# Down products as seven block products per pair of tiles, with GpSimd making the weight sums and part of the low parts

## What is computed

```python
def mlp(h, w_up, w_down):
    return jnp.square(jax.nn.relu(h @ w_up)) @ w_down
```

## Time and profile before

| | us |
|---|---|
| median of 3 runs | 1792.21 (1791.98 to 1797.71) |
| span of the profiled execution | 1793.1 |
| PE busy | 1736.8 (97%), 15035 matmuls |
| DVE busy | 954.7 (53%) |
| ACT busy | 548.6 (31%) |
| POOL busy | 159.4 (9%) |
| first MLP, second MLP after its root | 397.0 each |

### The profile page before, as it was taken

One profiled execution on the slowest core, in us unless ns is written; L12 is line 12 of the kernel. 1 busy time (PEld: TensorE's weight loads), 2 busy tenths in 40 slices (PEclk: granted clock), 3 DMA queues, 4 the chain that ended last, 5 costly groups with the idle time before them and its releaser, 6 DMA issues.

```text
span 1793.1 us, 36785 instructions
## 1 busy us (share of the span) xinstructions
PE 1736.8 (97%) x15035; PEld 1623.3 (91%) x15035; DVE 954.7 (53%) x1454; ACT 548.6 (31%) x1075; POOL 159.4 (9%) x212
## 2 busy tenths in 40 slices
PE   7998999999999999999999999999999999999998
PEld 6995667899999999999898898878799999999998
DVE  4336776655353433444587774677665435343454
ACT  4114556432121222231511413443133212122222
POOL 0710000320000000020000000012012000000002
PEclk9999999999999999999999999999999999999999
DMA  8219999337676767544368678523033767422221
GB/s 277 71 50 363 351 353 346 124 118 257 234 257 234 257 233 257 187 131 158 96 198 284 211 253 274 197 83 102 33 121 120 278 227 260 173 79 88 75 91 55
DMA packets 167162, 338.82 MB, mean 189 GB/s; under 512 B 9178, under 2 KB 116500, under 8 KB 165437
## 3 DMA queue, kind: packets, MB, share of 16 engines
q1 hardware_dynamic: 164691, 249.74, 41.3%
q0 software_dynamic: 2240, 87.41, 13.0%
q10 hardware_dynamic: 114, 0.03, 0.0%
HBM read 324.36 MB, written 100.19 MB: 237 GB/s over the span
## 4 chain that ended last, share of the span: by engine, by line
PE 86%; DVE 7%; ACT 2%; DMA 2%; issue 1%; SPq 1%; ACTq 0%; DVEq 0%
PE pp L667 55%; PE pp L977 16%; PE pp L727 2%; PE pp L926 1%; DMA kvring<-in_cache_b_kv 1%; PE pp L741 1%; PE pp L761 1%; PE pp L1084 1%; PE pp L1131 1%; PE pp L1180 1%; PE pp L1109 1%; DVE stat L1668 1%; DVE pp L1666 1%; ACT e_p L2163 1%; DMA vring<-in_cache_d_kv 1%
## 5 line engine op out<-in xcount | busy, mean ns | idle before, releaser
L1943 ACT ACTIVATE whi<-raw 128x1024 fp32r<-128x1024 f32 x208 | 220.6, 1060 | 899.7 <-PE pp L667 687.7
L667 PE MATMUL pp<-a_hi,whi 128*128 128x288 f32 x1280 | 275.8, 297 | 1.0 <-DVE zbuf L1335 0.7
L667 PE MATMUL pp<-a_lo,whi 128*128 128x288 f32 x1280 | 274.6, 296 | 0.0
L667 PE MATMUL pp<-a_hi,wlo 128*128 128x288 f32 x1280 | 274.4, 296 | 0.0
L1292 DVE TENSOR_TENSOR wlo<-raw,whi 128x1024 fp32r<-128x1024 f32 x208 | 256.0, 1231 | 30.5 <-ACT whi L1943 30.4
L667 PE MATMUL pp<-b_hi,whi 128*128 128x288 f32 x1152 | 247.0, 296 | 0.0
L667 PE MATMUL pp<-b_lo,whi 128*128 128x288 f32 x1152 | 247.0, 296 | 0.0
L667 PE MATMUL pp<-b_hi,wlo 128*128 128x288 f32 x1152 | 246.9, 296 | 0.0
L1351 DVE TENSOR_TENSOR x<-x,pp 128x576 f32 (+1 forms) x80 | 60.4, 755 | 295.1 <-PE pp L667 284.0
L667 PEld LDWEIGHTS pp<-a_hi,whi 128*128 128x128 f32 x1280 | 206.6, 189 | 2.3 <-issue 1.7
L667 PEld LDWEIGHTS pp<-a_lo,whi 128*128 128x128 f32 x1280 | 206.7, 189 | 0.0
(11 more groups left out here) (304 smaller groups left out, 2062.9 us busy)
## 6 DMA issues: line engine op xcount, KB each, us to landing
kvring<-in_cache_b_kv SPq DMA_DIRECT2D x128, 512.0 KB, 5.6
out_new_d_sample<-in_cache_d_kv POOLq DMA_DIRECT2D x32, 2040.0 KB, 8.5
raw<-in_w_up SPq DMA_DIRECT2D x32, 1024.0 KB, 5.4
raw<-in_w_down SPq DMA_DIRECT2D x32, 1024.0 KB, 5.2
kring<-in_cache_d_kv SPq DMA_DIRECT2D x104, 256.0 KB, 3.3
vring<-in_cache_d_kv SPq DMA_DIRECT2D x104, 256.0 KB, 5.3
raw<-in_w_in_cd SPq DMA_DIRECT2D x24, 1024.0 KB, 5.2
out_new_d_sample<-in_cache_d_kv POOLq DMA_DIRECT2D x8, 2016.0 KB, 8.3
```

What stands on the lines that cost most here:

```text
L667: last = pe.matmul(acc_h[s][:, h, :], w[s][:, k, :], m[:, k, NH * h:NH * h + NH], start=(at_ == 0 and n == 0), stop=(at_ == KT_N - 1 and n ...
L1943: act.activation(whi_v[j], raw_v[q // 2][:, :, j, :], ACT.Copy).then_inc(whi_ready, 1)
```

## The change

The 8 output tiles of a down half are taken in 4 pairs. For a pair, the weights (8 k-tiles by 2 tiles) are seen as a 2 by 2 block matrix (halves of k, and the two tiles), and the squares as 2 by 2 (halves of k, halves of the tokens). The pair's result is formed by seven block products in place of eight. A block product is 4 k-tiles x 3 terms of 128x288, so 12 matmuls; a down half has 28 (`DOWN`), and a chunk 36 counted steps (`CHUNK`).

- Weights: four sums per pair of tiles (128x512 each), made by GpSimd (`sums`) from the raw buffer. The seven forms are split in high (ACT, `form_hi`) and low (DVE, `form_lo`) parts of 128x512 in six slots, four of which lie in the memory of the up tiles' weights.
- Squares: k-tile kk of the two halves is up tile 2kk and 2kk+1. DVE makes four sums t1 to t4 of 128x288 for each pair of up tiles. The seven forms' high parts are ACT's (`squares_hi`). The low parts are GpSimd's for the first three pairs of up tiles (`squares_lo` under POOL) and DVE's for the last. DVE's square of the next even tile waits until the low parts of the pair before are made (b_ready).
- Reading: DVE adds each product's bank to a half tile of x as soon as the product is done (`read`, 28 of 128x288). Some products go on accumulating in a bank that has been read, so PE waits for the read two products back.
- Order on DVE at the end of the up half: after tile 6's square, two low parts and the low parts of forms 0 to 3, then tile 7's whole work, read 0, forms 4 to 6, and from there read m and form m+6 in turn.
- SP loads a down unit of 256 columns when the up weights in its buffer are split, so the first when the low part of tile 5 is made, the second after tile 7's, the third after form 6, the fourth after form 13.
- GpSimd's queue in a chunk: copy, low parts of pair 0; copy, low parts of pair 1; copy, weight sums 0, low parts of pair 2; copy, weight sums 1; then with the down half's copies weight sums 2 and 3.
- The finishing of output tiles moves to pairs: tiles 0 to 5 within the last down half, 6 and 7 after its last product.
- Some semaphores are merged and the counts moved; the work outside the MLPs stays.

```diff
-T_CD = T_M0 + 64
+CHUNK, DOWN = 36, 28
+T_CD = T_M0 + 4 * CHUNK
+PRODUCTS = ((None, 0, 0), (2, 5, 2), (1, 4, 0), (None, 2, 1), (0, 1, 0), (None, 6, 2), (3, 3, 0))
+SUM_READY = (2, 3, 1, 4)
+SLOT = [(m + 4) % 6 for m in range(24)] + [4, 5, 2, 3]
+FORM_AFTER = {m: m + 6 for m in range(20)} | {22: 26, 23: 27}
...
+                def steps(m, ks):
+
+                    p = m % 7
+                    f, s_ = PRODUCTS[p][1], SLOT[m]
+                    for k in ks:
+                        for n, (w, b) in enumerate(((f_hi_v, bf_hi), (f_hi_v, bf_lo), (f_lo_v, bf_hi))):
+                            last = pe.matmul(product_bank(m), w[s_][:, k, :], b[:, f, k, :],
+                                             start=(k == 0 and n == 0 and p in (0, 1, 3)),
+                                             stop=(k == 3 and n == 2), skip_group_check=(p in (2, 4, 5, 6)))
+                    return last
+
+                def down(c):
+
+                    w_ready = lambda m: pe.wait_ge(wlo_ready, in_chunk(t0, c, 8 + m + 1))
+                    reads = lambda m: pe.wait_ge(acc_free, in_chunk(t0, c, 8 + m + 1))
+                    squares = lambda n: pe.wait_ge(b_ready, c * 20 + (B_BASE[L] + 15 + n))
+                    w_ready(0)
+                    reads(0)
+                    squares(1)
+                    steps(0, range(4)).then_inc(tile_done, 1)
+                    w_ready(1)
+                    reads(1)
+                    steps(1, range(3))
+                    w_ready(3)
+                    steps(3, range(3))
+                    reads(2)
+                    steps(2, range(3))
+                    squares(4)
+                    for m in (1, 2, 3):
+                        steps(m, (3,)).then_inc(tile_done, 1)
+                    squares(5)
+                    for m in range(4, DOWN):
+                        w_ready(m)
+                        reads(m)
+                        steps(m, range(4)).then_inc(tile_done, 1)
...
+                def up_tile(c, u, first):
+
+                    j, kk = u % 2, u // 2
+                    z = zbuf[:, N * j:N * j + N]
+                    dve.wait_ge(tile_done, in_chunk(t0, c, u + 1))
+                    if first:
+                        rms(1 + 2 * L)(t0 // 4, 2)
+                    dve.tensor_tensor(z.rearrange("p (h c) -> p h c", h=2), acc_h[j], r_h, ALU.mult).then_inc(acc_free, 1)
+                    dve.wait_ge(acc_free, in_chunk(t0, c, u + 3))
+                    if j == 0:
+                        dve.wait_ge(b_ready, c * 20 + (bb + 5 * kk))
+                    dve.scalar_tensor_tensor(out=sqbuf[:, N * j:N * j + N], in0=z, scalar=0.0, in1=z, op0=ALU.max,
+                                             op1=ALU.mult).then_inc(sq_up, 1)
+                    dve.wait_ge(sq_up, c * 8 + (32 * L + u + 1))
+                    made = c * 16 + (64 * L + 4 * kk)
+                    b11, b12, b21, b22 = sq_h[0][:, 0, :], sq_h[0][:, 1, :], sq_h[1][:, 0, :], sq_h[1][:, 1, :]
+                    t1, t2, t3, t4 = (b_sum[:, n, :] for n in range(4))
+                    if j == 0:
+                        dve.tensor_tensor(t1, b12, b11, ALU.subtract).then_inc(b_sums, 1)
+                        if u < 6 and not first:
+                            tile_lo(c, u + 2)
+                        if kk == 3:
+                            squares_lo(c, kk, 1, 0, b11)
+                            squares_lo(c, kk, 2, 1, t1)
+                        if u == 6:
+                            for m in range(4):
+                                form_lo(m, c)
+                        return
+                    dve.wait_ge(b_sums, made + 1)
+                    dve.tensor_tensor(t2, b22, t1, ALU.subtract).then_inc(b_sums, 1)
+                    dve.tensor_tensor(t3, b22, b12, ALU.subtract).then_inc(b_sums, 1)
+                    if u < 7:
+                        tile_lo(c, u + 2)
+                    if kk == 3:
+                        squares_lo(c, kk, 3, slice(2, 4), sq_h[1])
+                    dve.wait_ge(b_sums, made + 2)
+                    dve.tensor_tensor(t4, b21, t2, ALU.subtract).then_inc(b_sums, 1)
+                    if u == 7:
+                        read(0, c)
+                    if kk == 3:
+                        squares_lo(c, kk, 4, slice(4, 6), b_sum[:, 1:3, :])
+                        squares_lo(c, kk, 5, 6, t4)
...
+                    for m in (4, 5, 6):
+                        form_lo(m, c)
+                    for m in range(1, DOWN):
+                        read(m, c)
+                        if m in FORM_AFTER:
+                            form_lo(FORM_AFTER[m], c)
...
+            def sums(L, t0, c, i):
...
+                w, s_ = raw_q[i % 2], w_sum[i % 2]
+                a11, a12, a21, a22 = w[:, :, 0, 0, :], w[:, :, 1, 0, :], w[:, :, 0, 1, :], w[:, :, 1, 1, :]
+                pool.tensor_tensor(s_[2], a11, a21, ALU.subtract).then_inc(w_sums, 1)
+                pool.tensor_tensor(s_[0], a21, a22, ALU.add).then_inc(w_sums, 1)
+                pool.wait_ge(w_sums, done + 2)
+                pool.tensor_tensor(s_[1], s_[0], a11, ALU.subtract).then_inc(w_sums, 1)
+                pool.wait_ge(w_sums, done + 3)
+                pool.tensor_tensor(s_[3], a12, s_[1], ALU.subtract).then_inc(w_sums, 1)
+
+            def squares_lo(L, c, kk):
+
+                for n, forms, src in ((1, 0, sq_h[0][:, 0, :]), (2, 1, b_sum[:, 0, :]), (3, slice(2, 4), sq_h[1]),
+                                      (4, slice(4, 6), b_sum[:, 1:3, :]), (5, 6, b_sum[:, 3, :])):
+                    pool.wait_ge(bhi_ready, c * 20 + (B_BASE[L] + 5 * kk + n))
+                    pool.tensor_tensor(bf_lo[:, forms, kk, :], src, bf_hi[:, forms, kk, :].bitcast(F32),
+                                       ALU.subtract).then_inc(b_ready, 1)
+
+            def chunk(L, t0, c, beside_up, beside_down):
+
+                for u in (0, 2, 4, 6):
+                    if beside_up:
+                        pool.wait_ge(tile_done, in_chunk(t0, c, u + 1))
+                        beside_up(u // 2)
+                    if u >= 4:
+                        sums(L, t0, c, u // 2 - 2)
+                    if u < 6:
+                        squares_lo(L, c, u // 2)
```

More of the change, by code:

```diff
@@ L698, in mlp @@
+                for u in range(8):
+                    up_tile(0, u, u == 0)
+                    if u == 0:
+                        mean_square(1 + 2 * L)()
+                down(0)
                 with pe.Fori(1, 4) as c:
[L699 to L700 removed]
+                    for u in range(8):
+                        up_tile(c, u, False)
+                    down(c)
@@ new lines, in chunk @@
+                def chunk(c, first=False, last=False):
+                    for u in range(8):
+                        up_tile(c, u, first and u == 0)
+                    for m in range(DOWN):
+                        act.wait_ge(tile_done, in_chunk(t0, c, 8 + m + 1))
+                        if m in FORM_AFTER:
+                            form_hi(FORM_AFTER[m], c)
+                        if m == 24 and not (last and L == 1):
+                            tile_hi(c, CHUNK)
+                        if m == 27 and not last:
+                            tile_hi(c, CHUNK + 1)
+                        if last and m in (7, 14, 21):
+                            finish_tiles(m // 7 - 1)
+                    if last:
+                        finish_tiles(3, (lambda: split_hi(T_CD // 4, 1)) if L == 0 else None)
@@ L2002, in token_major @@
+                if L == 1:
+                    act.wait_ge(vout, 16 * V_STORES[3])
+                chunk(0, first=True)
+                with act.Fori(1, 3) as c:
+                    chunk(c)
+                chunk(3, last=True)
             def token_major(T, parts=range(5)):
@@ new lines, in widest, with middle, narrow @@
+            def widest(b):
+                return lambda q: piece(2, b, QROWS * q, QROWS, QROWS * 1024 // 32)
+            def middle(b):
+                return lambda q: piece(1, b + q, 0, WIN[1] - TS, (WIN[1] - TS) * 1024 // 32)
+            def narrow(q):
+                if q < 2:
+                    dst, src = kept(0)
+                    copy(dst[4 * q:4 * q + 4, 0:WIN[0] - TS, :], src[4 * q:4 * q + 4, TS:WIN[0], :])
+            pool.wait_ge(vout, 16 * V_STORES[0])
+            with pool.Fori(0, 3) as c:
+                chunk(0, T_M0, c, widest(c * 2), widest(c * 2 + 1))
@@ L2487, in _ @@
             sum_squares(3)
[L2488 to L2497 removed]
+            pool.wait_ge(vout, 16 * V_STORES[3])
+            chunk(1, T_M1, 0, widest(NB - 1), middle(0))
+            chunk(1, T_M1, 1, middle(4), narrow)
+            chunk(1, T_M1, 2, None, None)
+            chunk(1, T_M1, 3, None, None)
             sum_squares(4, KT_N - 1)
```

289 lines of the change are left out of this document (193 added, 96 removed).

## The result

The changed kernel takes 1835.18 us (median of 4 runs, 1823.91 to 1836.87), the kernel before 1792.26 us beside it: ratio 1.0219 [1.0188, 1.0249] (ratios here are of the means of the runs). The sign and the kind of loss are as forecast; the size is not: +43 us where +16 were forecast. The time lies 0.8 us inside the upper end of the range and outside the forecast's own 1796 to 1822. One run of the variant sums_small took 1876.38 us, at a granted clock of 0.847 where its others have 0.99, and is left out of its median.

A forecast was written before the change was run, and what follows sets the result against it. TensorE, busy 97%, was taken as the bound: 1793.1 - 51.2 saved + 8 x 6.5 for waits + 8 x 1.5 for clock + 3 for ends = 1808.9, so 1808 us against the runs' median; own range 1796 to 1822, 8-in-10 range 1765 to 1836.

The forecast's parts named there:

- The saving: Down halves: 336 matmuls instead of 384 per chunk, 133.3 ns each, 51.2 us saved over 8 chunks.
- rival 1: Down halves: GpSimd stays out of DVE's way, loss about 2.4 us per chunk, no clock drop, 1763 us; chance 15%.
- The shared resource: SBUF access: a DVE instruction with two SBUF inputs and a GpSimd one take turns, one whole instruction each.
- The sequence of a steady chunk: One chunk from its first matmul: product 4 starts at 64.1 us against 57.6 unbroken, a loss of 6.5 us.
- both terms of a chunk, 6.5 and 1.5: Each chunk: 6.5 us lost by product 4 to the late schedule, plus 1.5 us for the clock.
- each GpSimd copy is issued a little later, and no one waits for it: GpSimd's queue: later issue of its copies was taken to delay nobody.
- one price for all transfers: Down weight loads: each pair lands 5.2 us after its raw buffer is freed.
- Ends: After the last product: one more ScalarE square and GpSimd sum, 2 us at the end, 1 at the first MLP's.
- ScalarE's extra pieces hidden in its idle 69%: ScalarE: 28 pieces of 0.61 us in place of 8 of 1.06 were taken to cost no time.
- the price of GpSimd's sums: GpSimd's 512-wide weight sums: 1.04 us with inputs in one tensor, 1.29 with two; four take 4.7 us with gaps.
- Rival 3: Up half: GpSimd bounds it, tile 7 stops too, full clock drops follow, 11 us per chunk, 1833 us; chance 15%.
- The clock: TensorE's waits around products 0 to 4 bring half clock: 1.5 us per chunk, between 0 and 3.4.

The follow-up runs named there:

- sums_small: Changed kernel with GpSimd's weight sums on 2 of 128 columns, the raw block used in their place (output not the reference's): 1776.26 us, ratio 0.9906.
- gpsimd_clear: Changed kernel with narrow_cut, low_dve and sums_small together (output not the reference's): 1763.88 us, ratio 0.9837.
- form_psum: Changed kernel with each weight form's low part computed from a PSUM bank in place of its high part (low parts wrong): 1807.72 us, ratio 1.0074.
- all4_halves: all4 with each GpSimd weight sum of 512 as two instructions of 256: 1784.41 us (median of 7 runs), ratio 0.9961.
- narrow_cut: Changed kernel with the kept cache's two 1920 KB copies cut into eight pieces of 480 KB: 1824.39 us, ratio 1.0168.
- finish_late: Changed kernel with ScalarE's squares of finished tiles 2 to 5 moved behind all forms' high parts: 1833.98 us, ratio 1.023.
- three_moves: all4 without finish_late: 1790.96 us, ratio 0.9991.
- all4: Changed kernel with narrow_cut, low_dve, finish_late, and the second pair's weight sums held until the first product is done: 1787.68 us, ratio 0.9973.
- low_dve: Changed kernel with all low parts of the squares' forms on DVE, none on GpSimd: 1814.85 us, ratio 1.0114.

## Why the prediction was wrong in size

**Right.** The saving: 384 matmuls fewer, and 98.1 us per chunk once GpSimd is out of the way, where the prediction's rival 1 had 98.4 (96.0 + 2.4), and 1763 us for the kernel against the 1763.88 of gpsimd_clear. The shared resource: form_psum takes only DVE's second SBUF input away, and the forms there take 684 ns on average in both their groups (224). The sequence of a steady chunk: wlo 7 forecast at 44.0 and done at 44.6; third pair's low parts 47.7 and 48.2; fourth form 56.1 and 57.1; product 4 at 64.1 and 65.7; chunk 104.0 and 104.6. Product 4's start holds both terms of a chunk, 6.5 and 1.5: it comes 8.1 us after the 57.6 of an unbroken stream. The Trainium skill ("SBUF — State Buffer", section "SBUF: two separate sides") has the shared pair held for a whole instruction; all4_halves agrees, 807 ns beside 256-wide neighbours against 925 beside 512-wide ones.

**Wrong, first: "each GpSimd copy is issued a little later, and no one waits for it", and one price for all transfers.** The prediction took the median of 5.2 us for every weight transfer. Nobody waits for the copies themselves, but two weight units land in 17.0 and 17.2 us beside the two 1920 KB copies. Before, this chunk had such units too (15.4 and 16.2 us), and they were hidden, because a raw buffer was free again as soon as its own two tiles were split, and so the next unit was asked for early. Now a buffer is held until the seventh form of its pair, and the next sums wait on the transfer's landing. Price: 14.1 us in one chunk, 10.8 in the whole (narrow_cut). The sum charged every chunk alike and had no such term, although the trace of before shows both slow copies and both slow units, behind a median.

**Wrong, second: the term "Ends", 2 + 1 us.** It looked at what comes after the last product, and not at what the finishing does inside the last down half. There the extra work costs 5.3 and 3.9 us over a steady chunk (109.9 - 104.6, 108.5 - 104.6), and after it the end costs 2.7. "ScalarE's extra pieces hidden in its idle 69%" is the sentence that failed: ScalarE had the time, but its order put the next form's high part behind a square that waited for GpSimd. finish_late and three_moves show ScalarE's share (1.8 and 2.4 us in the two MLPs alone, 2.5 in each once the rest is mended), and sums_small that nearly all of it hangs on the weight sums. How the rest divides between DVE's a_lo turns and GpSimd's lateness stays open.

**Wrong, at little cost: the price of GpSimd's sums.** The prediction took 1.04 us where both inputs lie in one tensor. The two such sums (L2701, L2702) take 1.26 and 1.28 us at least, like the other two (1.29 and 1.28), so all four stand at its upper price. The group still ends at 41.5 us of the chunk, where 41.2 was forecast.

**The remainder.** The forecast had 8 x (6.5 + 1.5) + 3 = 67 us of costs against 51.2 saved; measured is 91 (39.8 + 51.2). Of the 24 us missing, 13.6 are the chunk with the late transfers (118.2 - 104.6) and 9.2 the last chunks. Some 6.5 are the other excesses over the forecast: 1.4 in the second chunk of MLP 1, 0.8 in the first of MLP 2 (which took 104.0 us before, with the wait for its root), 0.6 or 0.7 in each of the other five, long ones included, 0.5 up to the end of the first, 0.7 at the end. That is 29; the stages between the MLPs gave back about 5. From the last down matmul of MLP 1 to the first up matmul of MLP 2 it is 572.2 us before and 567.8 after, where the forecast had 1 us more, and 567.9 to 573.7 in the eleven variants. Differences of this size come and go between executions; their cause was not looked for.

**Rival 3** (1833 us) came nearest in number and for another reason: the up half does stop ahead of tile 7 in four chunks, by 0.7 us, but a steady chunk is 104.6 us and not 107. The nearness is chance.

**The clock.** Forecast 1.5 us per chunk, between 0 and 3.4. Half clock totals 67 us after, 39 in all4, 26 in all4_halves, 19 in gpsimd_clear and 16 before. On the chain through chunk 3 it shows in one piece: 30 matmuls in 5.91 us, where gpsimd_clear has 30 in 3.98, so 1.9 us. In low_dve, chunks of the same code with 0, 3.4 and 6.6 us of half clock take 101.3, 101.3 and 103.6 us; in form_psum they take 101.1 with none and 104.0 with 6.8. So nothing to some 3 us per chunk goes with it. But a longer wait could bring both the half clock and the longer chunk, and no experiment held the waits and changed the clock, so its own share is not shown.

## What to carry to other kernels

A share of busy time says whether an engine can carry added work, not whether it can carry it in that order: price each GpSimd instruction by the DVE instruction that it meets (two SBUF inputs, or one in PSUM) and by what is queued behind it. Here GpSimd's low parts cost 20 us and its weight sums 59, each measured alone, and the matmuls saved were worth 51. When a buffer is held longer, look at the slowest landing of its transfers, not at the median, and at what runs beside it. And take the chunks that carry extra work (the last one) through the schedule by themselves.

## What the runs showed of the hardware

- DVE with two SBUF inputs and GpSimd take turns even for small shapes: a 128x288 addition of 0.46 us took 1.68. With one input in PSUM nothing of the kind appears (forms of 0.684 us on average, 224 of them).
- Two copies of 1920 KB that moved their packets about four at a time landed after 21.7 and 22.7 us; copies of 2016 and 2040 KB, about sixteen packets at a time, in 8.8 and 8.3 (medians). Two 1 MB weight loads of another queue beside the 1920 KB copies landed in 17.0 and 17.2 us, where the median is 4.9. With the same bytes in eight copies of 480 KB, about sixteen packets at a time and issued at four points, the weight loads there took 4.9 to 8.3. The form is the likely cause, but was not changed by itself.
